# Products of constants that nobody reads, at the block heads and in the last steps of the attention

## What is computed

```python
xn = rmsnorm(xp, norm_g[l])
u, gc, q, k, v, ga, iq, ik, iw = project(xn, w_in[l])
u_ext = jnp.pad(u, ((0, 0), (CONV_W - 1, 0), (0, 0)))
cy = conv_branch(u_ext, conv_w[l], conv_b[l], conv_ln_g[l], conv_ln_b[l])
o_blk = lax.map(lambda a: sparse_attend(a[0], a[1], a[2], a[3], k, v, ik, rel_bias, topk_p),
                (to_blocks(q, L_pad, n_blk), to_blocks(iq, L_pad, n_blk),
                 to_blocks(iw, L_pad, n_blk), pos_blocks))
...
xp = xp + merge(cy, gc, o, ga, w_out[l])
...
def sparse_attend(q, iq, iw, qpos, k_all, v_all, ik_all, rel_bias, topk):
    s = jnp.einsum('bthd,bsd->bths', iq.astype(jnp.float32), ik_all.astype(jnp.float32))
    score = jnp.einsum('bth,bths->bts', iw.astype(jnp.float32), jax.nn.relu(s))
    ...
    _, idx = lax.top_k(score, topk)
    ...
    p = jax.nn.softmax(logits, axis=-1)
```

## Time and profile before

| | us |
|---|---|
| median of 3 runs | 1704.01 |
| lowest and highest | 1702.09, 1707.3 |
| the profiled execution | 1701.9 |
| its span, first to last instruction | 1700.2 |
| TensorE busy in it | 1513.3 |
| VectorE, ScalarE, GpSimd busy | 1003.3, 697.9, 415.0 |
| mean granted TensorE clock | 0.96 |

### The profile page before, as it was taken

One profiled execution on the slowest core, in us unless ns is written; L12 is line 12 of the kernel. 1 busy time (PEld: TensorE's weight loads), 2 busy tenths in 40 slices (PEclk: granted clock), 3 DMA queues, 4 the chain that ended last, 5 costly groups with the idle time before them and its releaser, 6 DMA issues. The chain is left out here.

```text
span 1700.2 us, 28238 instructions
## 1 busy us (share of the span) xinstructions
PE 1513.3 (89%) x10647; PEld 1292.1 (76%) x10647; DVE 1003.3 (59%) x2123; ACT 697.9 (41%) x1238; POOL 415.0 (24%) x270
## 2 busy tenths in 40 slices
PE   5688989989998789999799999999999887569998
PEld 5686979978998769999577777776767665348886
DVE  3342998878988879888443444445455555333222
ACT  4354513253112352232225545556556654344331
POOL 2111224431115803222221001112222233043220
PEclk9999999999999999999879999999999999779999
DMA  7742365221357602224561513511111112295542
GB/s 237 219 107 50 68 92 119 67 75 54 84 161 222 157 22 72 70 75 125 163 156 36 115 37 79 113 35 34 39 45 50 58 61 77 81 231 162 173 149 93
DMA packets 183355, 172.71 MB, mean 102 GB/s; under 512 B 58956, under 2 KB 155348, under 8 KB 182700
## 3 DMA queue, kind: packets, MB, share of 16 engines
q1 hardware_dynamic: 176572, 152.91, 33.7%
q10 hardware_dynamic: 6136, 16.95, 3.4%
q0 software_dynamic: 512, 1.05, 0.2%
HBM read 109.35 MB, written 58.19 MB: 99 GB/s over the span
## 5 line engine op out<-in xcount | busy, mean ns | idle before, releaser
L845 PE MATMUL psum<-xh,wh 128*128 128x384 f32 (+1 forms) x1040 | 345.4, 332 | 23.1 <-ACT hst L782 11.5
L845 PE MATMUL psum<-xl,wh 128*128 128x384 f32 (+1 forms) x1040 | 341.6, 329 | 0.0
L845 PE MATMUL psum<-xh,wl 128*128 128x384 f32 (+1 forms) x1040 | 341.6, 328 | 0.0
L1436 ACT ACTIVATE pts<-psT 128x512 f32<-128x512 f32 (+1 forms) x302 | 167.1, 572 | 255.1 <-PE psT L1717 232.2
L845 PEld LDWEIGHTS psum<-xh,wh 128*128 128x128 f32 x1040 | 197.6, 190 | 26.4 <-ACT hst L782 15.2
L1606 DVE CUSTOM_DVE_ANT_0 L<-psU,mask 128x512 f32<-128x512 f32 (+3 forms) x260 | 143.5, 592 | 114.6 <-PE psU L1711 113.3
L1733 PE MATMUL psO<-pts,vs 128*64 128x128 f32 x2176 | 180.3, 287 | 27.2 <-ACT pts L1436 27.2
L845 PEld LDWEIGHTS psum<-xl,wh 128*128 128x128 f32 x1040 | 197.8, 190 | 0.0
L845 PEld LDWEIGHTS psum<-xh,wl 128*128 128x128 f32 x1040 | 197.5, 190 | 0.0
L995 DVE TENSOR_SCALAR_CACHE_REDUCE hit<-scores,T 128x1792 bf16<-128x1792 f32 (+8 forms) x120 | 184.6, 1538 | 11.7 <-issue 0.9
L693 POOL TENSOR_TENSOR wl<-uw,wh 128x1024 fp32r<-128x1024 f32 x44 | 121.5, 2762 | 276.8 <-ACT wh L730 276.8
(11 more groups left out here) (269 smaller groups left out, 2507.5 us busy)
## 6 DMA issues: line engine op xcount, KB each, us to landing
uw<-in_w_in SPq DMA_DIRECT2D x28, 512.0 KB
uw<-in_w_in SPq DMA_DIRECT2D x32, 256.0 KB
qt<-d_q SPq DMA_DIRECT2D x16, 512.0 KB, 4.0
xst<-in_x_prompt SPq DMA_DIRECT2D x15, 512.0 KB, 4.0
xr<-in_x_prompt SPq DMA_DIRECT2D x15, 512.0 KB, 4.4
out_y_prompt<-fin SPq DMA_DIRECT2D x15, 512.0 KB, 3.0
gate<-d_ga SPq DMA_DIRECT2D x17, 256.0 KB, 4.4
d_mix<-mix SPq DMA_DIRECT2D x17, 256.0 KB, 2.2
```

Of the source, the lines that this page charges most:

```text
L845: last = nc.tensor.matmul(u[:, 0:k * P], a[:, w % 2, cc, :], x[:, s0:s0 + k, cc, :], start=(cc == 0 and e == 0), stop=(cc == KC - 1 and e ...
L1436: A.activation(out, src, ACT.Copy).then_inc(act_pt, 1)
```

## The change

A helper makes n products of the constants, 256 columns each, into a place in PSUM that is free. It is called in five places, each with its waits. Nothing else changes; line numbers move (L390 to L397, L887 to L898, L1717 to L1731, L1763 to L1777, L2095 to L2115).

```diff
--- before.py
+++ after.py
@@ -171,6 +171,13 @@
     for n in pages:
         v = page_no(eng, ptab, n, cache)
         eng.dma_start(dst[:, n, :], cache[0, bass.ds(v, 1)].rearrange(layout)).then_inc(pages_in, 16)
+
+
+def spare_products(pe, cst, out, n):
+
+
+    for _ in range(n):
+        pe.matmul(out, part(cst, "ident"), cst[:, 0:256], start=True, stop=True)
 
 
 def project_norm_and_keys(nc, t, mem):
@@ -404,6 +411,10 @@
                     pe.wait_ge(nat_done, i + 1)
                     last = nc.tensor.transpose(u[:, 0:128], natst[:, i % 2, 256:384], ident)
                 last.then_inc(pe_job, 1)
+            n = len(J.jobs)
+            pe.wait_ge(act_job, n - 3)
+            pe.wait_ge(dve_job, J.count(n - 3, ("xT", "ikT")))
+            spare_products(nc.tensor, mem.cst, psum[:, n % 4, 0:256], 5)
 
 
 INDEXER = [("iq", 0), ("iq", 1)]
@@ -900,6 +911,9 @@
                     nc.tensor.matmul(u[SROW:SROW + NS, 0:PAST], ws[:, :], srelu[:, 0:PAST], start=True, stop=True)
                     last = nc.tensor.matmul(u[SROW:SROW + NS, PAST:LS], ws[:, :], srelu[:, PAST:LS], start=True, stop=True)
                 last.then_inc(pe_job, 1)
+            arrived(len(jobs) - 4)
+            pe.wait_ge(mask_ready, sum(len(g) for g in GROUPS) - 2)
+            spare_products(nc.tensor, mem.cst, psum[:, len(jobs) % 4, 0:256], 8)
 
         @block.vector
         def _(dve):
@@ -1787,6 +1801,8 @@
             for p, (i, j) in enumerate(pairs):
                 if p + 1 < NP_:
                     logits(p + 1)
+                if i < 2:
+                    spare_products(T, mem.cst, take_pt(("T", p, *groups(p)[0]))[:, 0:256], 2)
                 pe.wait_ge(exp_done, sides_before(p + 1))
                 if p == 0:
                     pe.wait_ge(ri_ready, 1)
@@ -1822,6 +1838,8 @@
                         mean_of(("V", k), s2[:, k % 2, 0:norm_count(k)], norm_count(k))
                 for k in range(len(NORM)):
                     if TURN_STEP[k] == p:
+                        if k == len(NORM) - 2:
+                            spare_products(T, mem.cst, take_pt(("Y", k, NORM[k][0]))[:, 0:256], 8)
                         pe.wait_ge(yn_done, k + 1)
                         for i in NORM[k]:
                             turn(k, i)
@@ -2077,6 +2095,8 @@
         @block.tensor
         def _(pe):
             T = nc.tensor
+            pe.wait_ge(swish_in, 1)
+            spare_products(T, mem.cst, O[:, 0, 0:256], 10)
             n = 0
             for what, k in schedule:
                 if what == "tile":
```

## The result

| | kernel before | changed kernel |
|---|---|---|
| median | 1702.78 us (5 runs) | 1711.19 us (5 runs, 1708.81 to 1715.82) |
| profiled execution, span | 1700.2 us | 1707.2 us |
| ratio | | 1.0046, 95% interval 1.0028 to 1.0064 |

The prediction was 1703.0 us, with a range up to 1708.7. The time lies above it. One execution of e7 (4877 us) and one of the kernel before (3567 us) are left out of all ratios.

What follows compares the result with a forecast made beforehand. Four blocks run in sequence, with TensorE's clock dipping at block heads and the attention's end. Terms summed to -0.1 us on 1701.9; 2.1 for the median and -1 for edit 4 gave 1703 us, range 1697.5 to 1708.7.

Steps and rivals of the forecast that it cites:

- edit 2: Eight products at the end of stage 2, inside TensorE's wait; clock low again at stage 3's start: 0 us.
- rival (b): Slower: pair products stand in the last pairs' path, where the clock would be high anyway: 1710.2 us, chance 0.11.
- Edit 1: Five products at the end of stage 1, beside the output DMA; stage 2 starts at the high clock: -2.9 us.
- Edit 3: Eight products before the last but one turn of the norms, in TensorE's wait; that turn runs fast: -1.5 us.
- Edit 4: Two products in each of the eight last pairs; clock stays high, but products stand on the path: +2.2 us.
- Edit 5: Ten products at the head of stage 4; tile 0 ends earlier, tile 1 waits longer and starts low: +2.1 us.

Runs made afterwards that it cites:

- e7: Only edits 2 and 3 added to the kernel before: 1706.23 us, 1.0006.
- e16: The whole change plus 51 tiny products, making 257 more instructions ahead of stage 3, against the kernel before: 1709.34 us, 1.0023.
- e6: Only edit 2 added to the kernel before: 1706.51 us, 1.0022.
- e5: Only edit 3 added to the kernel before: 1704.24 us, 1.0004.
- e1: Only edit 4 added to the kernel before: 1706.64 us, 1.0008.
- e4: Only edit 5 added to the kernel before: 1706.23 us, 1.0009.
- e13: Only edits 1 and 2 added to the kernel before: 1713.22 us, 1.0043.
- e14: The 13 products of edits 1 and 2 made tiny (one column), same 54 instructions, against the kernel before: 1712.49 us, 1.0051.
- e15: Edits 1 and 2 plus 51 tiny products, 257 more instructions ahead of stage 3, against the kernel before: 1706.19 us, 1.0006.
- e18: Edits 1 and 2 with the mask's load issued ahead of qt and gate, against the kernel before: 1693.77 us, 0.9936.
- e3: Only edit 1 added to the kernel before: 1705.65 us, 1.0022.
- e17: The kernel before with only the mask's load issued ahead of qt and gate: 1693.25 us, 0.9942.

## Why the prediction was wrong

- **The step that failed** is the one that cost the added instructions: each product was priced by its time on TensorE alone (edit 2 at nothing, since it lies in a wait). The instructions have a second price, in the place of every later fetch. This price of edits 1 and 2 is as large as the whole result: 1.0051 for the instructions alone, 1.0043 for both edits, 1.0006 for both with the fetches put back. No rival had it. Beside it some terms were mis-sized: as measured below, the five edits add up to -2 + 0 + 0 + 3.3 + 1.2 = +2.5 us, not -0.1. With the fetches put back the whole change still lost 1.0023 (e16), some 4 us, one of them to the filling. The range ended at 1708.7 because all its bounds were products and clock levels; rival (b) came near the time (1710.2) by luck, with reasons that are not those found.
- **Edit 1 (-2.9 us)**: the mechanism holds. The scores start 18.7 to 18.8 us after the stage in every trace with the products. But the kernel before had the longest of the starts without them (21.7; others 20.1 to 21.5), so the term was too large. Up to its last mask stage 2 took 706.3 us in the mean of the ten traces with edit 1 and 708.1 in the ten without: some 2 us. (The two profiled executions differ by only 0.5 there, since that of the kernel before, at 704.3, was a short one.) Alone the edit lost 0.22%, with two of the mask's loads over 1 us longer.
- **Edit 2 (0)**: right on the clock, which was low at the head of stage 3 all the same (830.95 to 841.19 us); its 33 instructions cost (e6: 1.0022).
- **Edit 3 (-1.5 us)**: wrong. In the changed kernel the wait left was 2.82 us, not 2.0, and the level fell again. Alone (e5) it was 1.79 us, the turn of group 7 ran high as forecast (2.05 us), and from there to the last turn e5 took 18.7 us against 19.3 to 20.7 without the edit; but the last turn then ran low (3.60 us, not 2.05). Nothing is left in the time (1.0004).
- **Edit 4 (+2.2 us)**: the level stayed high and a pair took 3.4 us, both as forecast. From the last turn on it cost 3.3 us in e1, within its bounds of 0 to 4.7; the time shows 1.0008.
- **Edit 5 (+2.1 us)**: 1.2 us in stage 4 (e4), by the fall behind the wait of tile 1 as described, though that wait was 2.95 us and not 4.0; the time shows 1.0009. The fall is not this edit's alone: e1 and e13, which do not have it, took 191.4 and 191.2 us there, each with a low stretch (from 1524 and from 1531 us on).

Open: why TensorE's level stays low behind the last turn in all three traces with edits 1 and 2 and no pair products, which is the larger part of the loss in e14's trace. Its waits there are the same 0.53 to 0.75 us a pair as at the high level. The runs show that it goes with the place of the fetches (gone in e15) and with the order of the loads (gone in e18), not by which step. The traces show one thing more: in these three and in e5 the level falls at the last turn itself, and then again 10 to 11 us behind it; in the nine other traces without pair products that keep the old order of loads, and in e18, it holds for some 22 us behind the turn. What makes it fall at that turn is not shown: the wait of 1.4 us ahead of it stands as well in traces where the turn ran high (the kernel before, e4, e6, e15). Each kernel has one trace, but over all its executions the mean granted clock is lower in e13 than in e15 (0.957 and 0.960), and in e14 than in the kernel before (0.954 and 0.958). Nor is it settled what e3 and e6 lose alone (both 1.0022 [1.0005, 1.0039], against [0.9993, 1.0014] of the unchanged kernel).

## What to carry to other kernels

An instruction can cost more than its time: here, adding 54 to TensorE's 21,732 moved all its later fetches, each a packet of 16 KB that took 0.88 to 1.91 us in the 20 traces, and some of them into loads in flight. So when a small edit in a wait makes a kernel slower far away from it, compare the landing times of the loads in both traces, and repeat the edit with the same number of instructions that do nothing. Then cure the load, not the edit: of loads issued together, let the one that is waited for go first. Here that was worth 0.6%, over twice what all gains of the prediction's sum came to.

## What was not expected of the hardware

- One fetch of 16 KB (0.92 to 1.82 us for its packet) made loads of 160 to 256 KB in flight land 1.1 to 2.4 us later (the mask's 3.9 to 4.5 us became 5.0 to 6.2; `gate` 6.7 in e18 instead of 4.3 in e17). From 1250 us on, in all 18 traces with the old order, a fetch 0.7 to 3.0 us after the mask's issue went with a load of 5.0 us or more, and one 3.1 to 4.0 us after it, at the end of the packets, with one of 3.8 to 4.7.
- 54 instructions, 0.25% of TensorE's program, cost 0.5% of the time; 203 more took it back.
